# Fused hybrid encoder layer on one core: x is turned by products with a diagonal of inverse roots, and the first two in-projection tiles run side by side

## What is computed

```
h = concatenate([meta, x])                      # 272 x 2048
u = rmsnorm(h, attn_norm)                       # h * rsqrt(mean(h*h) + EPS) * attn_norm
glu_a, glu_b, qkv, z, beta, decay = split(u @ w_in)        # w_in: 2048 x 6160
y_conv  = conformer_conv(glu_a, glu_b, ...)     # 31-tap causal convolution, group norm, silu
y_delta = gated_deltanet(qkv, z, beta, decay, ...)         # chunked recurrence, 8 heads of 128
h = h + concatenate([y_conv, y_delta]) @ w_out
u = rmsnorm(h, ffn_norm)
h = h + hier_moe(u, ...)      # 32 experts, w_gate, w_up: 2048 x 512 each, w_down: 512 x 2048
out = rmsnorm(h, final_norm)[16:]
```

## Time and profile before

| | |
|---|---|
| three executions | 1561.31, 1562.98, 1563.0 us (median 1562.98) |
| profiled execution, its own time | 1562.8 us |
| its span, first to last instruction | 1560.9 us |
| TensorE busy | 1530.8 us (98%) |
| TensorE weight loads busy | 841.1 us (54%) |
| VectorE busy | 523.7 us (34%) |
| ScalarE busy | 229.5 us (15%) |
| mean load rate over the span | 307 GB/s |

### The profile page before, as it was taken

One profiled execution on the slowest core, in us unless ns is written; L12 is line 12 of the kernel. 1 busy time (PEld: TensorE's weight loads), 2 busy tenths in 40 slices (PEclk: granted clock), 3 DMA queues, 4 the chain that ended last, 5 costly groups with the idle time before them and its releaser, 6 DMA issues.

```text
span 1560.9 us, 19575 instructions
## 1 busy us (share of the span) xinstructions
PE 1530.8 (98%) x8086; PEld 841.1 (54%) x8086; DVE 523.7 (34%) x1110; ACT 229.5 (15%) x481; POOL 55.6 (4%) x58
## 2 busy tenths in 40 slices
PE   8999999999999999999999999999999999999997
PEld 6888777777876445444344344434434434434432
DVE  2466347743484114131221321321321321321323
ACT  2002313222222203010100100000000000000003
POOL 0000021002020000000000000000000000000000
PEclk9999999999999999999999999999999999999999
DMA  9653331141236036899999999999999999999996
GB/s 349 198 176 129 108 109 55 55 154 63 109 109 244 26 134 278 355 402 423 409 428 429 429 430 427 428 430 429 428 428 429 430 429 427 428 429 429 430 427 263
DMA packets 71160, 479.54 MB, mean 307 GB/s; under 512 B 11681, under 2 KB 20402, under 8 KB 42674
## 3 DMA queue, kind: packets, MB, share of 16 engines
q1 hardware_dynamic: 70816, 478.55, 74.9%
q10 hardware_dynamic: 290, 0.23, 0.1%
HBM read 476.66 MB, written 2.10 MB: 307 GB/s over the span
## 4 chain that ended last, share of the span: by engine, by line
PE 79%; DMA 15%; DVE 3%; ACT 1%; issue 1%; SPq 0%; ACTq 0%; POOL 0%; DVEq 0%
PE bank L1070 24%; PE bank L741 20%; DMA ring<-in_w_up_dram 12%; PE bank L1095 9%; PE bank L889 7%; PE bank L1150 5%; PE bank L1032 5%; DMA ring<-in_w_down_dram 2%; PE bank L1088 1%; PE bank L827 1%; PE bank L810 1%; DVE region_m L1698 1%; PE bank L830 1%; DMA rows<-in_conv_ln_b_dram 0%; PE bank L686 0%
## 5 line engine op out<-in xcount | busy, mean ns | idle before, releaser
L1070 PE MATMUL bank<-ring,region_m 128*64 128x512 f32 x2048 | 453.1, 595 | 3.9 <-DMA ring<-in_w_up_dram 3.8
L741 PE MATMUL bank<-region_u,ring 128*128 128x272 f32 (+2 forms) x1536 | 371.2, 395 | 0.0
L741 PEld LDWEIGHTS bank<-region_u,ring 128*128 128x128 f32 x1536 | 284.9, 191 | 52.8 <-issue 0.9
L1070 PEld LDWEIGHTS bank<-ring,region_m 128*64 128x64 f32 x2048 | 142.2, 137 | 276.9 <-issue 268.4
L1095 PE MATMUL bank<-region_qy,region_s 128*64 128x512 f32 x992 | 218.4, 592 | 0.5 <-issue 0.5
L1095 PEld LDWEIGHTS bank<-region_qy,region_s 128*64 128x64 f32 x992 | 71.6, 137 | 140.7 <-issue 137.8
L1932 DVE TENSOR_TENSOR region_s<-region_s,bank 64x512 f32<-64x512 f32 x32 | 22.1, 692 | 356.5 <-ACT region_s L1436 356.5
L1032 PEld LDWEIGHTS bank<-region_m,region_u 128*128 128x128 f32 x960 | 108.4, 192 | 12.2 <-issue 12.2
L1150 PE MATMUL bank<-region_m 128*128 128x512 f32 x256 | 114.1, 599 | 0.0
L1032 PE MATMUL bank<-region_m,region_u 128*128 128x128 f32 x960 | 111.2, 277 | 0.0
L1698 DVE SCALAR_TENSOR_TENSOR region_m<-region_qy,cols,region_m 128x256 f32<-128x256 f32 x240 | 108.7, 517 | 2.1 <-DVE region_qy L1726 1.0
(11 more groups left out here) (264 smaller groups left out, 827.4 us busy)
## 6 DMA issues: line engine op xcount, KB each, us to landing
region_qy<-in_w_down_dram SPq DMA_DIRECT2D x62, 2048.0 KB, 19.7
ring<-in_w_gate_dram SPq DMA_DIRECT2D x59, 2048.0 KB, 17.2
ring<-in_w_up_dram SPq DMA_DIRECT2D x59, 2048.0 KB, 21.6
ring<-in_w_in_dram SPq DMA_DIRECT2D x40, 1024.0 KB, 7.1
ring<-in_w_out_dram SPq DMA_DIRECT2D x12, 1024.0 KB, 5.4
ring<-in_w_gate_dram SPq DMA_DIRECT2D x9, 1024.0 KB, 7.6
ring<-in_w_up_dram SPq DMA_DIRECT2D x9, 1024.0 KB, 10.2
ring<-in_w_in_dram SPq DMA_DIRECT2D x16, 512.0 KB, 4.9
```

The lines of the kernel that those rows point to most:

```text
L741: last = mm(banks[n % 2][:, 0:width], slot[s][:, 512 * k + P * j:512 * k + P * (j + 1)], uT[:, 4 * g + k, T - width:T], start=g == k == 0, ...
L1070: last = mm(banks[x_][CAP * v:CAP * (v + 1), :], uTe[:, 4 * g + k, CAP * x_:CAP * (x_ + 1)], w_gu[v][:, k0:k0 + 512], start=g == k == 0, s ...
```

## The change

- The diagonals: VectorE no longer multiplies x and the meta rows. It multiplies the identity by the inverse roots of 128 rows (`take_rstd`: one 16 x 16 for the meta rows, one 128 x 128 for each half of x, in `region_h`) and raises `diag_ready`. TensorE then makes `x_piece.T @ diagonal` as an ordinary float32 product in place of the transpose.
- The sums of squares change engines: the meta rows' is now ScalarE's, that of x rows 0 to 127 is VectorE's and stands first on its engine.
- `N_FIRST` is 2: TensorE and VectorE wait for the identity and `attn_norm` alone, and only these 16 rows are turned early. The other 41 columns are turned in `turn_rows` by one more transpose of all 57 rows, and copied by one more copy in `take_rows`; `N_ROWS` is 8.
- Banks: the meta rows go to bank 1 and the groups to banks 2 to 6, so that bank 0 and bank 1 take the first two tiles.
- Tiles 0 and 1 run side by side: four products of tile 0 and four of tile 1 for each piece g.
- The copies that are issued, their order and their sizes stay as they are.

```
-N_FIRST, N_ROWS, N_LATER = 7, 3, 10
+N_FIRST, N_ROWS, N_LATER = 2, 8, 10
...
+        diag_x = [region_h[:, 1024 + P * t:1024 + P * (t + 1)] for t in range(TT)]
+        diag_m = region_h[0:META, 1024 + P * TT:1024 + P * TT + META]
...
             pe.wait_ge(first_loaded, 16 * N_FIRST)
-            tr(banks[7][:, 0:57], rows[0:57, 0:P], ident[0:57, 0:57]).then_inc(cols_turned, 1)
-
-            pe.wait_ge(x_normed, 1)
+            tr(banks[7][:, 0:16], rows[0:16, 0:P], ident[0:16, 0:16]).then_inc(cols_turned, 1)
+
+            pe.wait_ge(diag_ready, 1)
             for k in range(KD):
-                last = tr(banks[6][:, META * k:META * (k + 1)], m_in[:, P * k:P * (k + 1)], ident[0:META, 0:META])
+                last = mm(banks[1][:, META * k:META * (k + 1)], m_in[:, P * k:P * (k + 1)], diag_m, start=True, stop=True)
             last.then_inc(x_turned, 1)
...
-                pe.wait_ge(x_normed, 2 + 2 * t + g // 2)
+                if g == 0:
+                    pe.wait_ge(diag_ready, 2 + t)
...
-                    last = tr(bk[1 + i % 5][:, k, :], x_in[:, t, P * (4 * g + k):P * (4 * g + k + 1)], ident)
+                    last = mm(bk[2 + i % 5][:, k, :], x_in[:, t, P * (4 * g + k):P * (4 * g + k + 1)], diag_x[t],
+                              start=True, stop=True)
...
                 pe.wait_ge(rows_loaded, 16 * N_ROWS)
+                tr(banks[7][:, 0:57], rows[0:57, 0:P], ident[0:57, 0:57])
...
             steps = delta()
+            for _ in zip(*(project(n, TILES[n][2], TILES[n][3], T) for n in range(2))):
+                pass
             for n, (kind, ch, b, j) in enumerate(TILES):
+                if n < 2:
+                    continue
...
+            act.wait_ge(meta_loaded, 16)
+            own.then(act_fn(region_h[0:META, D:], m_in, ACT.Square, accum_out=ssq[0:META, 0:1]))
+            own.settle()
+            rstd_of(0, META)
             act.wait_ge(x_squared, 1)
-            rstd_of(0, META)
-            act.wait_ge(x_loaded0, 16)
-            own.then(act_fn(junk, x_in[:, 0, :], ACT.Square, accum_out=ssq[:, 1:2]))
-            own.settle()
             rstd_of(1, P)
...
+            dve.wait_ge(x_loaded0, 16)
+            stt(out=junk, in0=x_in[:, 0, :], scalar=1.0, in1=x_in[:, 0, :], op0=ALU.mult, op1=ALU.mult,
+                accum_out=ssq[:, 1:2]).then_inc(x_squared, 1)
+
+            def take_rstd(n, diag, m):
+
+                dve.wait_ge(rstd_ready, n + 1)
+                ts(diag, ident[0:m, 0:m], rstd[0:m, n:n + 1], None, ALU.mult).then_inc(diag_ready, 1)
+
+            dve.wait_ge(first_loaded, 16 * N_FIRST)
+            dve.wait_ge(warm_zeroed, 1)
+            take_rstd(0, diag_m, META)
+            take_rstd(1, diag_x[0], P)
             dve.wait_ge(cols_turned, 1)
-            dve.tensor_copy(cols[:, 0:57], banks[7][:, 0:57]).then_inc(cols_ready, 1)
-            dve.wait_ge(rstd_ready, 1)
-            ts(m_in, m_in, rstd[0:META, 0:1], None, ALU.mult).then_inc(x_normed, 1)
...
+            dve.tensor_copy(cols[:, 0:16], banks[7][:, 0:16]).then_inc(cols_ready, 1)
...
                 dve.wait_ge(cols_turned, 2)
+                dve.tensor_copy(cols[:, 16:57], banks[7][:, 16:57])
```

More of the change, by code:

```diff
@@ L368, in hybrid_kernel @@
         logit_part = sem("logit_part")
-        x_normed = sem("x_normed")
+        diag_ready = sem("diag_ready")
         x_squared = sem("x_squared")
@@ L1224, in rstd_of @@
                 act_fn(rstd[0:m, i:i + 1], lnt[0:m, i:i + 1], ACT.Exp, scale=-0.5).then_inc(rstd_ready, 1)
[L1226 to L1231, removed]
+            rows_of = ((ffn_norm, 16), (delta_norm_g, 32), (conv_dw_b, 33), (conv_ln_g, 41), (conv_ln_b, 49))
+            act.dma_start(m_in, meta).then_inc(meta_loaded, 16)
+            act.dma_start(ident, cst_in[:, 0:P]).then_inc(first_loaded, 16)
+            act.dma_start(rows[0:16, 0:P], attn_norm[0].rearrange("(r n) -> r n", n=P)).then_inc(first_loaded, 16)
+            for a, r in rows_of:
+                act.dma_start(rows[r:r + a.shape[1] // P, 0:P], a[0].rearrange("(r n) -> r n", n=P)).then_inc(rows_loaded, 16)
+            act.wait_ge(meta_loaded, 16)
+            own.then(act_fn(region_h[0:META, D:], m_in, ACT.Square, accum_out=ssq[0:META, 0:1]))
+            own.settle()
+            rstd_of(0, META)
             act.wait_ge(x_squared, 1)
-            rstd_of(0, META)
-            act.wait_ge(x_loaded0, 16)
-            own.then(act_fn(junk, x_in[:, 0, :], ACT.Square, accum_out=ssq[:, 1:2]))
-            own.settle()
             rstd_of(1, P)
@@ L1249, in _ @@
                 for k in range(4):
-                    last = act_fn(uT[:, 4 * g + k, META + P * t:META + P * (t + 1)], bk[1 + i % 5][:, k, :], ACT.Copy,
+                    last = act_fn(uT[:, 4 * g + k, META + P * t:META + P * (t + 1)], bk[2 + i % 5][:, k, :], ACT.Copy,
                                   scale=g_attn[:, 4 * g + k:4 * g + k + 1])
@@ L1520, in step @@
                 own.settle()
-            dve.wait_ge(meta_loaded, 16)
-            stt(out=region_h[0:META, D:], in0=m_in, scalar=1.0, in1=m_in, op0=ALU.mult, op1=ALU.mult,
-                accum_out=ssq[0:META, 0:1]).then_inc(x_squared, 1)
-            dve.wait_ge(cols_turned, 1)
-            dve.tensor_copy(cols[:, 0:57], banks[7][:, 0:57]).then_inc(cols_ready, 1)
-            dve.wait_ge(rstd_ready, 1)
-            ts(m_in, m_in, rstd[0:META, 0:1], None, ALU.mult).then_inc(x_normed, 1)
[L1530 to L1535, removed]
+            dve.wait_ge(x_loaded0, 16)
[8 more added lines that the diff above has]
+            take_rstd(1, diag_x[0], P)
+            dve.wait_ge(cols_turned, 1)
+            dve.tensor_copy(cols[:, 0:16], banks[7][:, 0:16]).then_inc(cols_ready, 1)
             def take_x(i):
@@ L1540, in take_x @@
                 dve.wait_ge(x_turned, 2 + i)
-                tt(uT[:, 4 * g:4 * g + 4, META + P * t:META + P * (t + 1)], bk[1 + i % 5], b4(g_attn[:, 4 * g:4 * g + 4]), ALU.mult
+                tt(uT[:, 4 * g:4 * g + 4, META + P * t:META + P * (t + 1)], bk[2 + i % 5], b4(g_attn[:, 4 * g:4 * g + 4]), ALU.mult
                    ).then_inc(ut_dve, 1)
-            normalise(0)
             dve.wait_ge(cols_ready, 1)
             dve.wait_ge(x_turned, 1)
-            tt(uT[:, :, 0:META], banks[6][:, 0:KD * META].rearrange("p (k n) -> p k n", n=META),
+            tt(uT[:, :, 0:META], banks[1][:, 0:KD * META].rearrange("p (k n) -> p k n", n=META),
                g_attn.unsqueeze(2).to_broadcast([P, KD, META]), ALU.mult).then_inc(ut_dve, 1)
@@ L1550, in _ @@
             take_x(1)
-            normalise(1)
+            take_rstd(2, diag_x[1], P)
             for i in UT_BY_DVE[2:]:
```

## The result

| | before | changed |
|---|---|---|
| median of 8 executions each | 1562.35 us | 1566.53 us |
| lowest and highest | 1560.18 to 1563.35 | 1564.02 to 1568.80 |
| profiled execution, own time (span) | 1562.8 (1560.9) | 1565.43 (1563.5) |
| first tile starts (profiled execution) | 20.77 | 22.91 |

The change makes the kernel slower: ratio 1.003, interval 1.0021 to 1.0039, so 3.3 to 6.1 us. The forecast was 1564.3 and "no difference that can be told" with 0.73; the range held the time. The executions of the changed kernel also lie wider apart (4.8 us against 3.2), and they sort by the granted clock over their whole span: 0.997 in the two fastest (1564.02 and 1565.43), 0.994 in the three slowest (1568.03 to 1568.80).

The account below looks back on a forecast made before the run. TensorE's products were taken to bound the kernel, so the first tile's start sets the end. A 1.4 us loss from products, net of the earlier start, plus 0.1 for later rows, on 1562.8 gave 1564.3 us; range 1561.3 to 1567.0.

Parts of the forecast that it names:

- That 1 us at the first tile is 1 us at the end: Whole kernel: later stages follow TensorE's progress, so a shifted first tile shifts the end by the same amount.
- Part 1, the start: Kernel's opening: shorter wait and no multiplying of meta rows start the meta turns at 10.3 instead of 12.96, gaining 2.6 us.
- Part 2, the price of products: Turns of meta rows and x: products take 0.22 to 0.23 us at full clock, x's 0.43 at half clock.
- my own fall at 13.1: During the meta turns: TensorE's clock was taken to fall at 13.1 us, as in the kernel before.
- Part 2, the clock: Turns of x: full clock back at 16.5, 3.4 us after its fall; first tile at 22.2, loss 1.4 us.
- my slower rival: Turns of x: clock low until 19.9 or longer; at 19.9, +3.3 us in all, 1566.1 us; chance 0.20.
- Part 3: Feeding and draining the turns of x: second root and VectorE's reads come in time, so nothing gained or lost.
- Part 4: Tiles 0 and 1 side by side: no piece of `w_in` would be late anyway, so nothing gained or lost.
- Part 5: Rows turned later, after tile 2: one more transpose costs +0.1 us, bounds 0.1 and 0.3.
- The rival with a shorter fall at 269: Low clock at 269.1 us also missed: up to 1.7 us saved, 1561.4; chance 0.28 shared with no early fall.
- The factor four between product and transpose: Turns of x: rival that a float32 product costs four transposes, 7 us more, 1571 us; chance 0.01.

Follow-up runs that it names:

- experiment 9: Experiment 7's kernel with tiles 0 and 1 one after the other instead of side by side: 1559.38 us, ratio 0.9983.
- experiment 4: The changed kernel with the meta rows' products moved between the two halves of x, so wide products come first: 1566.65 us, ratio 1.0031.
- experiment 11: The changed kernel run once more, unaltered, for a second look at its executions: 1567.06 us (three executions), ratio 1.0034.
- 1: The changed kernel with tiles 0 and 1 one after the other again: 1567.11 us, ratio 1.0031.
- experiment 6: The changed kernel without diagonal products: ScalarE normalises the meta rows, VectorE x in halves, all turns are transposes: 1558.54 us, ratio 0.9981.
- 5: The changed kernel with the meta rows normalised by ScalarE and turned by transposes, x still by products: 1560.86 us, ratio 0.9995.
- experiment 10: Experiment 7's kernel with the meta rows alone turned by narrow products with a diagonal: 1564.03 us, ratio 1.0009.
- experiment 7: Experiment 6's all-transpose kernel with eight products of zeros ahead instead of six: 1558.11 us, ratio 0.9977.
- experiment 3: The changed kernel with the wait for all seven copies put back and all 57 rows turned at once: 1567.82 us, ratio 1.0037.
- 8: The changed kernel with eight products of zeros instead of six: 1566.05 us, ratio 1.0029.

## Why the prediction failed

**That 1 us at the first tile is 1 us at the end: right.** Own time less start of the first tile is 1542.0 us for before (1562.8 less 20.77), and lies between 1541.4 and 1542.8 in all profiled executions but that of experiment 9 (1544.2), while the first tile moves from 16.05 to 26.73. It holds to about 1 us, then, not to tenths.

**Part 1, the start: right.** `attn_norm` seen at 10.13 (taken: 10.1), meta products from 10.40 (10.3).

**Part 2, the price of products: right at full clock, mis-sized for narrow ones in the low stretch.** In a stretch at full clock (17.5 to 22.5) 47 records of x's products lie in 5 us, those cut by its edges counted, so close to the 0.22 us for a product of two that was taken. The narrow ones cost 0.23 at full clock as taken (3.68 us for 16 in experiment 4, 14.17 to 17.85), but 0.43 at half clock, the same as wide ones. I had priced all 16 at full clock, though my own fall at 13.1 stood before their end at 14.0: the four or so behind it cost 0.8 us more by my own prices, which would have put the first tile some 0.5 us later. And I wrote nothing for the case that the clock falls sooner.

**Part 2, the clock: here it failed.** The step "before, it came after 6.8 us [...] the turns are now products, so I take the second: back at 16.5" took the length of the low stretch from the row whose work looked nearest, and took one execution for all. The runs show that the stretch is 3.4, 6.8 and 10.2 us long in executions of this same opening (change, 11, 1), and begins between 12.05 and 13.8. Where it begins early, narrow products run inside it, at 0.43 us, and it lasts longer (the table above). The sum for a median execution follows from the first point: 1566.53 less 1542.5 gives a first tile at 24.0. That is, to 0.1 us, the first tile of my slower rival (the clock back at 19.9; 1566.1), to which I gave 0.20. The forecast described the profiled execution (22.2 against 22.91) and the rival came close to the median one. So close a match is luck: the rival kept the fall at 13.1 and all narrow products at full clock, while the profiled execution nearest to the median, that of experiment 11, had the clock low from 12.4 to 19.2 and 3.2 us of narrow products in it.

**Why there was no gain from the earlier start.** The runs split the 4.2 us, each against its own kernel before. Up to experiment 6 (loads, exchanged sums, meta rows normalised off the path, side by side) -3.3; x's products +2.3 (5 against 6); narrow products for the meta rows +5.1 (the changed kernel against 5). These are steps of one ladder, so their sum is the loss by construction; the largest has its own check in experiment 10 (+5.6). I had put the narrow products at +1.9 us (3.7 against 1.84) and saw in them the bystanders of the low clock. About 2.8 us of the 5.1 are their length alone: in the profiled executions of the change and of 5 the low stretch is 3.4 us in both, and the first tile stands at 22.91 and 20.10. The rest goes with a lower clock (over the whole span 0.994 to 0.997 in the change's executions, 0.996 to 0.998 in those of 5). That narrow products are what holds the clock down fits all the stretches in the table, but no experiment set the moment of the fall, so it is argued and not shown.

**Part 3: right**, no root or read held TensorE up. **Part 4: right**, side by side has no effect that can be told (1, 9). **Part 5:** the changed kernel's lag grows from 2.14 us at the first tile to 2.49 at 155 us, 0.25 of it where the rows are turned; 0.1 was taken, and 0.3 was the upper bound.

**The rival with a shorter fall at 269** gave 0.7 us in the profiled execution and not up to 1.7, because ScalarE's step behind the gap is late next.

**The factor four between product and transpose**, which the Trainium skill states ("TensorE: Matmul & The Clock Gate", Terms), is not borne out: 0.12 us for a transpose in experiment 7 (1.97 / 16) and 0.22 for a product. The same page's Part 4 says that the full clock doesn't engage for transposes. Here the clock stayed at 1.00 through 32 float32 transposes with a wait in between (experiment 7), and in the kernel before it came back at 19.9, with TensorE on transposes alone since 12.96, so the trace disagrees.

What stays open: why a low stretch begins where it does in a given execution. In the profiled executions of the changed kernel and of experiments 1 and 3 the zeros at the very start sped up at about 7.2, 5.4 and 4.7 us, and the fall came at 13.8, 12.05 and 11.4, in the same order; but that is three executions, and nothing here sets it. Whether the 1.9 us from before to 6 beyond the shorter wait (3.3 less 1.4) come from the exchanged sums or from the meta rows leaving VectorE was not separated.

## What to carry to other kernels

Price a product by a diagonal against the transpose that it replaces at both clocks, with its true count of records; a narrow one costs as much as a wide one (0.22 to 0.23 us), and where a low stretch overlapped a run of them, it lasted longer and the wide ones behind them paid too. Where a stretch sits near a change of the clock, one profiled execution is one draw: compare several, and put the start of the next fixed stage, not the span, beside each other. Take the cheap half of such a change: here the early wait, work moved to an idle engine and transposes kept gave 1558.1 us, 0.23% under the kernel before.

## What was not expected of the hardware

- TensorE's clock fell although TensorE had worked without a pause for some us: at 17.8 in experiment 4, with narrow products from 14.2 and wide ones before them; at 15.5 in 8, 1.4 us behind the narrow ones; at 13.8 in the change, 3.4 us after they began.
- Low stretches were the longer the more narrow turns ran in them: 3.4 us with at most 0.4 us of them, 6.8 with 1.7 to 3.2, 10.2 with 4.5 or more (eleven executions).
- A product with 16 columns costs 0.23 us at 2.4 GHz and 0.43 at 1.2 GHz, as much as one with 128. The weight loads, of 128 columns for both, filled the time (9.96 of 10.00 us at half clock in experiment 3), so it is likely these that set the price; no run varied their width.
- With the same instructions up to the first tile, the stretch at half clock lasted 3.4, 6.8 and 10.2 us in three executions (the change, 11, 1), and the time ranged over 4.8 us in eight executions of the changed kernel.
